# All projections of the mixers as three rounded passes of split weights

## What is computed

```
z = x @ w_in                                  # 1024 -> 9 blocks of 1024 and 8 gate columns
aq, af, ai, ag, bu, bv, bo, big, bfg, ga, gb = split(z)
o_a, s_new = hgrn2_scan(silu(aq), (1-lb)*sigmoid(-af), log_f, ai, state)   # branch A
y_a = (rms_norm_heads(o_a) * silu(ag)) @ w_pa
u   = silu(causal_conv(bu));  q_b, k_b = u @ w_q_blk, u @ w_k_blk
h_b, c_new, n_new, m_new = mlstm_scan(q_b, k_b, bv, big, log_sigmoid(bfg), states)  # branch B
y_b = (sigmoid(bo) * layer_norm_heads(h_b)) @ w_pb
out = (sigmoid(ga) * y_a + sigmoid(gb) * y_b) @ w_o
x   = layer_norm(ALPHA * x + out);  then the feed-forward part
```

## Time and profile before

| | us |
|---|---|
| three executions | 2596.16, 2597.39, 2619.27 |
| median | 2597.39 |
| the profiled execution: its own time | 2619.27 |
| its span, first to last instruction | 2617.5 |
| mixer of layer 0, first product of f to last of wo | 19.4 to 740 |
| dense part | 763 to 998 |
| mixer of layer 1 | 1016.5 to 1716 |
| experts, first to last pass | about 1778 to 2576 |

### The profile page before, as it was taken

One profiled execution on the slowest core, in us unless ns is written; L12 is line 12 of the kernel. 1 busy time (PEld: TensorE's weight loads), 2 busy tenths in 40 slices (PEclk: granted clock), 3 DMA queues, 4 the chain that ended last, 5 costly groups with the idle time before them and its releaser, 6 DMA issues.

```text
span 2617.5 us, 27956 instructions
## 1 busy us (share of the span) xinstructions
PE 2489.0 (95%) x11716; PEld 1926.7 (74%) x11716; DVE 1379.5 (53%) x1587; ACT 955.1 (36%) x1014; POOL 214.9 (8%) x183
## 2 busy tenths in 40 slices
PE   8999998999989998999989999979999999999996
PEld 5667486676669996667467676667888888888884
DVE  2533434712144431535354712148889889889894
ACT  2232122001033421332032011037667667667673
POOL 1312021300000000313021200000000000000000
PEclk9999958999989999999988999989999999999998
DMA  5121340632324433212340633239999999999990
GB/s 187 65 101 65 101 131 17 217 137 97 129 97 144 146 115 129 97 69 97 97 134 17 233 121 128 100 127 337 341 320 365 328 329 365 328 329 364 327 349 22
DMA packets 270588, 470.90 MB, mean 180 GB/s; under 512 B 13930, under 2 KB 106362, under 8 KB 270456
## 3 DMA queue, kind: packets, MB, share of 16 engines
q1 hardware_dynamic: 270364, 469.04, 51.5%
q10 hardware_dynamic: 92, 0.00, 0.0%
HBM read 439.10 MB, written 29.92 MB: 179 GB/s over the span
## 4 chain that ended last, share of the span: by engine, by line
PE 92%; DVE 4%; ACT 2%; issue 1%; SPq 0%; DMA 0%; POOL 0%; DVEq 0%; ACTq 0%; POOLq 0%
PE bank L508 27%; PE bank L456 9%; PE bank L458 9%; PE bank L457 9%; PE bank L522 6%; PE bank L464 3%; PE bank L463 3%; PE bank L462 3%; PE bank L546 3%; PE bank L743 2%; PE bank L752 2%; PE bank L802 2%; PE bank L609 2%; PE bank L778 1%; PE bank L600 1%; PE bank L619 1%
## 5 line engine op out<-in xcount | busy, mean ns | idle before, releaser
L508 PE MATMUL bank<-arena,weights 128*128 128x320 f32 x2560 | 712.3, 439 | 13.4 <-ACT arena L1095 7.6
L508 PEld LDWEIGHTS bank<-arena,weights 128*128 128x128 f32 x2560 | 490.7, 193 | 217.1 <-issue 9.3
L1552 DVE TENSOR_TENSOR unit_rest<-weights,unit_high 128x2048 fp32r<-128x2048 f32 x198 | 452.2, 2290 | 85.3 <-ACT unit_high L1133 84.7
L1133 ACT ACTIVATE unit_high<-weights 128x2048 fp32r<-128x2048 f32 x198 | 379.3, 1919 | 159.0 <-PE bank L458 153.6
L456 PE MATMUL bank<-unit_high,tokens_high 128*128 128x512 f32 (+1 forms) x768 | 290.5, 378 | 2.0 <-DVE tokens_rest L1558 2.0
L458 PE MATMUL bank<-unit_high,tokens_rest 128*128 128x512 f32 (+1 forms) x768 | 286.6, 373 | 0.0
L457 PE MATMUL bank<-unit_rest,tokens_high 128*128 128x512 f32 (+1 forms) x768 | 286.2, 373 | 0.0
L522 PE MATMUL bank<-weights,arena 128*128 128x512 f32 (+1 forms) x384 | 167.4, 593 | 0.0
L1552 DVE TENSOR_TENSOR unit_rest<-arena,unit_high 128x2048 fp32r<-128x2048 f32 x66 | 150.9, 2290 | 29.1 <-ACT unit_high L1133 29.0
L458 PEld LDWEIGHTS bank<-unit_high,tokens_rest 128*128 128x128 f32 x768 | 145.0, 189 | 25.9
L456 PEld LDWEIGHTS bank<-unit_high,tokens_high 128*128 128x128 f32 x768 | 145.1, 189 | 25.3 <-DVE tokens_rest L1558 2.1
(11 more groups left out here) (355 smaller groups left out, 3330.1 us busy)
## 6 DMA issues: line engine op xcount, KB each, us to landing
weights<-in_w_in SPq DMA_DIRECT2D x36, 2048.0 KB, 7.8
weights<-in_w_ex_gate SPq DMA_DIRECT2D x67, 1024.0 KB, 6.6
weights<-in_w_ex_up SPq DMA_DIRECT2D x66, 1024.0 KB, 6.5
weights<-in_w_ex_down SPq DMA_DIRECT2D x65, 1024.0 KB, 6.8
arena<-in_w_ex_down SPq DMA_DIRECT2D x23, 1024.0 KB, 6.5
arena<-in_w_ex_up SPq DMA_DIRECT2D x22, 1024.0 KB, 7.2
arena<-in_w_ex_gate SPq DMA_DIRECT2D x21, 1024.0 KB, 7.2
weights<-in_state_mlstm_c SPq DMA_DIRECT2D x8, 2048.0 KB, 8.3
```

Of the source, the lines that this page charges most:

```text
L508: mm = nc.tensor.matmul(out[:, 0:T], w[:, k, chunk(m)], src[:, k, :], start=k == 0, stop=k == KC - 1)
L1133: nc.scalar.activation(high[n % MOE_SPLIT], raw[n % MOE_RAW], ACT.Copy).then_inc(mo_high, 1)
L1552: nc.vector.tensor_tensor(rest[n % MOE_SPLIT], raw[n % MOE_RAW], high[n % MOE_SPLIT], ALU.subtract)\
```

## The change

Three things are changed together.

1. Weights. The strips of 2 MB become units of 1 MB (`mixer_units`): 256 columns of all 8 slices, or, for v and bv, 512 columns of 4 slices. The ring has four places. Each unit is split: ACT writes the rounded copy into one of three homes (`unit_high`), DVE overwrites the landed unit with the rest (`unit_rest`). There are 48 split units in a mixer. The states of the sampled tokens go through the same ring in 1 MB units, unsplit.
2. Inputs. `xT` is gone but for the last layer's end: the layer's input is kept as `xh` (rounded) and `xl` (the rest). The inputs of pa, pb and wo and the gate columns are split as well (`oAh`, `oAl`, `hBh`, `hBl`, `mgh`, `mgl`, `gwh`, `gwl`). The first residual adds both parts in two instructions of DVE instead of one.
3. Products. Each float32 product becomes three passes. A tile of v or bv is made in two steps, one for each unit, so v has 6 fillers of half the size.

Three functions of the experts are renamed (`unit_high` to `expert_high`, `unit_rest` to `expert_rest`); some temporaries have other places; the loads of the first feed-forward units wait for units of wo instead of strips.

```diff
-RING = 3
+RING = 4
+HOMES = 3
...
+def fillers(hf):
+    v = [("v", hf, m) for m in range(6)]
+    if hf == 0:
+        return v + [(n, i, m) for n, i in (("g", 0), ("f", 1), ("q", 1)) for m in range(4)]
+    return v + [(n, i, m) for n, i in (("g", 1), ("bu", 0), ("bu", 1)) for m in range(4)] + \
+        [("bv", i, m) for i in range(2) for m in range(6)]
...
+            def project(l, name, i, m, sh, sl, ready=None):
+                part = m // 2
+                wh, wl = [w.rearrange("p (k n) -> p k n", k=KC)[:, :, chunk(m % 2)] for w in split_at_home(l, name, i, part)]
+                if m % 2 == 0:
+                    pe.wait_ge(*dv_s.at("unit rest", l, name, i, part))
+                out = claim(pe, "G", l, name, i, m)[:, 0:T]
                 for k in range(KC):
-                    mm = nc.tensor.matmul(out[:, 0:T], w[:, k, chunk(m)], src[:, k, :], start=k == 0, stop=k == KC - 1)
+                    if ready is not None and i == 0 and m == 0:
+                        pe.wait_ge(*dv_s.at(ready, l, k))
+                    mm = turned_product(out, wh[:, k], wl[:, k], sh[:, k, :], sl[:, k, :], k == 0, k == KC - 1)
...
-                pe.wait_ge(*dv_s.at("oA", l))
-                project_all("pa", oA)
+                project_all("pa", oAh, oAl, "oA rest")
...
-                pe.wait_ge(*dv_s.at("merged", l, 7))
-                project_all("wo", merged)
+                project_all("wo", mgh, mgl, "merged rest")
...
+            def unit_high(l, w):
+                u = SPLIT[w]
+                place_, full, n = unit_at(l, *u)
+                act.wait_ge(full, n)
+                if w % FIRST_HALF >= HOMES or w == FIRST_HALF or w == FIRST_HALF + 1:
+                    act.wait_ge(*pe_s.at("unit", l, *SPLIT[w - HOMES]))
...
+                nc.scalar.activation(split_at_home(l, *u)[0], place_, ACT.Copy).then_inc(*ac_s.done("unit high", l, *u))
...
+            def evac(l, name, i, m):
+                take(l, name, i, m)
+                next_high(l, name, i, m)
...
+            def unit_rest(l, w):
+                u = SPLIT[w]
+                dve.wait_ge(*ac_s.at("unit high", l, *u))
+                wh, wl = split_at_home(l, *u)
+                nc.vector.tensor_tensor(wl, unit_at(l, *u)[0], wh, ALU.subtract).then_inc(*dv_s.done("unit rest", l, *u))
...
+            for t, (t0, r) in enumerate(TT):
+                for i in range(2):
+                    dve.wait_ge(*ac_s.at("xin high", t, i))
...
+                    ins.then_inc(*free(dv_s, 0, "xin", t, i))
...
             for l in range(DEPTH):
+                for w in range(1, 4 + HOMES):
+                    unit_rest(l, w)
                 for hf in range(2):
                     prepare(l, hf)
                     settle()
+                    given = 0
                     for lv in range(LEVELS):
                         operands(l, hf, lv)
                         collect(l, hf, lv - 1)
+                        given = rests(l, hf, given, lv)
                         settle()
...
                     hgrn_norm(b)
+                    if b > 0:
+                        hgrn_rest(b - 1)
+                unit_rest(l, FIRST_HALF)
...
+                    if m > 0:
+                        merged_rest(m - 1)
+                    next_rest("pb", m // 4, m % 4)
+                merged_rest(KC - 1)
...
-                        nc.vector.scalar_tensor_tensor(x1T[:, k, :], xT[:, k, :], ALPHA, of(l, "wo", i, m)[:, 0:T],
+                        nc.vector.scalar_tensor_tensor(x1T[:, k, :], xl[:, k, :], ALPHA, of(l, "wo", i, m)[:, 0:T],
...
+                        nc.vector.scalar_tensor_tensor(x1T[:, k, :], xh[:, k, :], ALPHA, x1T[:, k, :], ALU.mult, ALU.add)\
+                            .then_inc(*dv_s.done("res1", l, k))
```

More of the change, by code:

```diff
@@ L204, in build @@
         x1T = view(a_x1, KC, T)
-        ring = view(0, RING, SLOT, of=weights)
+        xh = rounded("tokens_in_high", 0, KC, T)
+        xl = rounded("tokens_in_rest", a_x1, KC, T)
+        ring = [view(i * UNIT, UNIT, of=weights) for i in range(RING)]
+        ring_rest = [rounded(f"mixer_rest{i}", i * UNIT, UNIT, base=weights_at) for i in range(RING)]
         par = view(place(KC * NPAR), KC, NPAR)
@@ L280, in build @@
         sW = [view(a_att + 896 + i * 448, 448) for i in range(2)]
-        kmB = [view(a_x1 + i * D, D) for i in range(2)]
+        kmB = [view(a_x + i * D, D) for i in range(2)]
         cvg = view(a_v, KC, 27)
@@ L513, in project_rows @@
-            def project_rows(l, name, i, t):
-                w, full, n = strip_at(l, name, i)
-                w = w.rearrange("p (k n) -> p k n", k=KC)
-                if t == 0:
-                    pe.wait_ge(full, n)
-                out = claim(pe, "G", l, name, i, t)
-                t0, r = TT[t]
-                for k in range(KC):
-                    mm = nc.tensor.matmul(out[0:r, :], xT[:, k, t0:t0 + r], w[:, k, :], start=k == 0, stop=k == KC - 1)
-                mm.then_inc(*pe_s.done("mm", l, name, i, t))
+                if m % 2 == 1:
+                    table[("pe", "unit", l, name, i, part)] = pe_s.count
@@ new lines, in project_rows @@
+            def project_rows(l, name, i, m):
+                part, t = divmod(m, 3)
+                t0, r = TT[t]
+                wh, wl = [w.rearrange("p (k n) -> p k n", k=4) for w in split_at_home(l, name, i, part)]
+                if t == 0:
+                    pe.wait_ge(*dv_s.at("unit rest", l, name, i, part))
+                if part == 0:
+                    claim(pe, "G" if t < 2 else "S", l, name, i, 3 + t)
+                out = of(l, name, i, 3 + t)[0:r, :]
+                for j in range(4):
+                    k = 4 * part + j
+                    mm = split_product(out, xh[:, k, t0:t0 + r], xl[:, k, t0:t0 + r], wh[:, j], wl[:, j], k == 0, k == KC - 1)
+                mm.then_inc(*pe_s.done("mm", l, name, i, m))
@@ L1341, in _, with hgrn_high @@
                 table[("act", "rsA", l)] = ac_s.count
+                def hgrn_high(h):
+                    act.wait_ge(*dv_s.at("oA", l, h))
+                    nc.scalar.activation(oAh[:, h, :], oA[:, h, :], ACT.Copy).then_inc(*ac_s.done("oA high", l, h))
+                for h in range(HA - 1):
+                    hgrn_high(h)
+                unit_high(l, FIRST_HALF)
                 act.wait_ge(*pe_s.at("interB", l, DB - 1))
@@ L1384, in _ @@
                     dense()
-                    norm(l, "2", x1T, xT)
+                    for w in range(HOMES):
+                        unit_high(l + 1, w)
+                    norm(l, "2", x1T, x1T)
                 else:
@@ L1723, in _ @@
                         nc.vector.memset(vTok[NS:P, 2, :], 0.0).then_inc(*dv_s.done("rows padded", l))
+                    else:
+                        dve.wait_ge(*ac_s.at("gates high", l))
+                        nc.vector.tensor_tensor(gwl, gw, gwh, ALU.subtract).then_inc(*dv_s.done("gates rest", l))
+                    given = rests(l, hf, given, 17)
                 dve.wait_ge(*ac_s.at("free", l, "bu", 1, 3))
@@ L1914, in _, with next_rest @@
                 table[("dve", "hB", l)] = dv_s.count
+                hgrn_rest(HA - 1)
+                unit_rest(l, FIRST_HALF + 1)
+                unit_rest(l, FIRST_HALF + 2)
+                def next_rest(name, i, m):
+                    for part in range(2):
+                        if m == last_step((name, i, part)) and SPLIT.index((name, i, part)) + HOMES < NSPLIT:
+                            unit_rest(l, SPLIT.index((name, i, part)) + HOMES)
                 for i in range(2):
@@ L1959, in _ @@
                     dve.wait_ge(ff_res, KC)
-                    norm(l, "2", x1T)
+                    norm(l, "2", x1T, (l + 1, 0))
+                    for k in range(KC):
+                        dve.wait_ge(*ac_s.at("x high 2", l, k))
+                        nc.vector.tensor_tensor(xl[:, k, :], x1T[:, k, :], xh[:, k, :], ALU.subtract)\
+                            .then_inc(*dv_s.done("x rest", l + 1, k))
                 else:
```

366 lines of the change are left out of this document (221 added, 145 removed).

## The result

The changed kernel takes 2521.84 us (median of four executions, 2520.31 to 2523.90), the kernel before 2596.77 (2595.30 to 2619.27). The ratio over all executions is 0.9695, with an interval of 0.9657 to 0.9734; by the medians it is 75 us less. The forecast was 2514 with a range of 2470 to 2568, faster with a chance of 0.88.

A forecast was written before the change was run, and what follows sets the result against it. TensorE, with 92% of the chain, was taken to bound the kernel. 158 us less work, minus 54 lost in the level loops, 17 in the last part and 3.6 at the start, gave 83 below a 2597.4 median: 2514, range 2470 to 2568.

## What to carry to other kernels

Work taken from the engine that bounds a kernel is gained in full only where the other engines' turn is no longer than the work that is left to it. Before a saving is counted, write out the turn in the other engines' queues, in order, and see what it takes without the bounding engine: here 12.2 us against the 12.2 that stood there.

A new instruction on a helper engine is dear by its place, not by its length. A rest of 2.29 us that waits for a landing cost nothing behind the instructions that free a bank, and up to 4.2 us ahead of them. Re-ordering alone was worth 63 us here, beside the 75 of the change itself.

When two executions of the same instructions differ by some 19 us, compare the granted clock stretch by stretch before looking for a cause in the code.

## What was not expected of the hardware

A gap of about 4 us ahead of the sampled tokens was followed by 24 us at a granted clock of 0.95 in one execution and by 44 us at 0.50 in another of the same kernel, with TensorE busy for 42.08 of them. In that execution a busy TensorE did not get the clock back.

An earlier start of 4.1 us gave no shorter time: level 1 fell to the lower clock (4.80 instead of 2.63 us) where it had not before. Gains of a few microseconds next to pauses were here within what the clock gives and takes.
